# A two-block transformer kernel on one core: residual stream and output projections turned channel-major, norm factors applied after the projections

## The chip, the cores and the metric

One core of one Trainium2 chip runs the whole program. The metric is the device time of one execution in microseconds, lower is better; a kernel's time is the median of its runs.

## What is computed

256 tokens of width 1024 pass through two blocks in fp32. The first block is a token mixer (four groups of 256 channels: softmax attention with forget gates, gated delta rule, two gated linear attentions) and a convolutional gated feed-forward. The second has two layers: a short-convolution mixer or differential attention, a convolutional feed-forward, and a gated per-layer embedding. Each sub-layer has a norm before it, and those of the second block one behind it too:

```python
x = x + mixed @ w_out                                   # first block
x = x + conv_glu_ffn(rms_norm(x, norm2_g), ...)
for i in range(2):                                      # second block
    h = rms_norm(x, g_pre_mix[i])
    mix = short_conv_mixer(h, ...) if i == 0 else diff_attention(h, k, v, ...)
    x = x + rms_norm(mix, g_post_mix[i])
    ffn = conv_ffn(rms_norm(x, g_pre_ffn[i]), ...)
    x = x + rms_norm(ffn, g_post_ffn[i])
    x = x + rms_norm(sigmoid(rms_norm(x, g_pre_ple[i]) @ w_gate) * (p[i] @ w_proj), g_post_ple[i])

def rms_norm(x, g):
    return x * rsqrt(mean(x * x, axis=-1) + EPS) * g
def conv_ffn(h, w_up, w_conv, w_down):
    gate, up = split(causal_dwconv(h @ w_up, w_conv), 2)    # 3 taps along the tokens
    return (silu(gate) * up) @ w_down
```

## The kernel before, in words

**The weight stream.** All weights go through the core as 160 blocks of 128 x 2048 floats (1 MB), three slots of a ring deep. SyncE loads a block into `raw`, ScalarE copies it to `w_hi` rounded to fp32r (`split` of the scalar program, L980 to L985), VectorE makes `w_lo` = raw - w_hi (`split` of the vector program, L1459 to L1461). Every product is three fp32r matmuls: hi x hi, hi x lo, lo x hi. TensorE counts used blocks in `block_used`. Block n shares a slot with block n - 3, so ScalarE may split block n once block n - 3 is used; `ahead(n)` on both engines splits block n + 2, at a place in the program that is written out by hand. TensorE waits for both parts in `block_ready`. There is no planner: each engine's order is the order of its code.

**Two kinds of block.** A column block holds 256 columns of a weight and all 1024 of its rows; `columns` (from L400) makes 2 x 8 x 3 matmuls of 256 columns from it. A row block holds 256 rows and all 1024 columns; `row_block` (from L429) makes 2 x 2 x 3 x 2 matmuls of 512 columns, with the tokens' chunk as the weight side and the block as the moving side, so that the result lies token-major in PSUM banks 0 to 3 (`low4`), the first token tile in banks 0 and 1.

**Norms.** `x` is token-major, 2 tiles of 128 tokens by 1024. `norm` lets ScalarE square and sum tile 0 (L1011), take the factor by logarithm and exponential (L999, L1000) and scale the tile into `xn` (L1013); VectorE does tile 1 (L1472, L1475). TensorE then turns both tiles by 16 transposes (`turn`, L461), ScalarE reads them with the gain into `h_hi` (L1028) and VectorE into `h_lo` (L1489). Only then the next column block can start. Post norms (`post`) do the same with the projection in PSUM: square and sum (L1346), factor, scale with the broadcast gain (L1954), add to x (L1957), tile by tile.

**Feed-forward.** 11 pairs of a gate and an up block, each with a row block of `w_down`. The loop has three blocks per pass: gate block of pair i, up block of pair i, row block of pair i - 1. Per pair ScalarE multiplies by the last convolution tap out of PSUM (L1274), VectorE adds the two older taps out of PSUM (L1866, L1870), ScalarE applies silu (L1285), VectorE multiplies (L1893), and the product is split into high (ScalarE, L1291) and low (VectorE, L1897). Between them both engines make the splits of the coming blocks.

**Mixer.** 15 column blocks, the first of which holds only 28 columns of gates; between and in the middle of them stand hand-placed pieces of the four mixers (`before` and `middle` lists of each engine). ScalarE rounds the masks (L1047) and makes the gates beside block 1; TensorE's sums of the gates stand before block 3. Three projections get convolution taps (L1552) and are turned in the middle of block 4 (L521).

**Attention.** Blocks k (4), q (4) and v (4, row blocks), with logits, softmax and transposed weights of one head at a time in the middle of the blocks; after the last block the head products, a norm of each head (L2040) and 16 transposes before the output projection.

**GpSimd** only issues DMAs here: tables, and six broadcasts of a post gain.

## Time and profile before

| | us |
|---|---|
| Median of 3 runs | 1187.96 (1186.85 to 1188.34) |
| Time of the profiled execution, first to last instruction (span) | 1187.9 |
| TensorE matmul busy | 1088.8 |
| VectorE busy | 753.8 |
| ScalarE busy | 589.0 |
| GpSimd busy | 8.8 |
| Mean granted TensorE clock, share of full | 0.945 |

The profile is one execution taken by the hardware profiler. A busy TensorE is not one at its peak: matmuls overlap, so the distance from one start to the next says more than a duration. In the timeline a row is: start, duration, engine, line, operation, output and inputs, shapes, count, and in brackets the idle time before it with what ended it. A line may be that of a helper: L390 is every matmul but those of the row blocks, which are L445.

### The profile page before, as it was taken

The page shows a single profiled execution, that of the slowest core. Times are in us where ns is not written, and L with a number is a line of the kernel's source. Part 1 is how long each engine was busy: PE and PEld are TensorE (multiplying, and loading weights), DVE is VectorE, ACT ScalarE, POOL GpSimd, SP SyncE. Part 2 cuts the span into 40 slices and gives each one's busy share as a digit, 9 for nine tenths or more (in the row PEclk, how much of TensorE's full clock was granted, in tenths as well). Part 3 has the DMA queues.
Part 4 walks back from the last instruction along what each step waited for, and adds up shares of the span by engine and source line. Part 5 has one row for each costly group of instructions (what it writes and reads, how often), then busy time and mean ns, then how long its engine had stood idle before and what let it go on. Part 6 is the DMA issues. An engine that isn't in the chain of part 4 may idle for free.

```text
span 1187.9 us, 19600 instructions
## 1 busy us (share of the span) xinstructions
PE 1088.8 (92%) x7748; PEld 997.1 (84%) x7748; DVE 753.8 (63%) x940; ACT 589.0 (50%) x788; POOL 8.8 (1%) x20
## 2 busy tenths in 40 slices
PE   5899987889999997998999999896996899999985
PEld 5899976769999996996999999676985699999964
DVE  5765535557667666656677666746586576676673
ACT  6643242246445545444545544645564555544563
POOL 0000000000000000001000000000000000000000
PEclk9999976699999998999899999997998999999998
DMA  8333310034555553456255554442441445555530
GB/s 352 128 107 107 107 36 1 2 111 158 197 181 176 201 184 125 163 203 244 94 209 177 195 191 177 159 153 89 175 148 66 159 143 181 202 175 184 178 123 35
DMA packets 25675, 178.00 MB, mean 150 GB/s; under 512 B 2925, under 2 KB 3077, under 8 KB 5024
## 3 DMA queue, kind: packets, MB, share of 16 engines
q1 hardware_dynamic: 24208, 172.54, 40.8%
q0 software_dynamic: 1424, 4.85, 1.3%
q8 instruction: 32, 0.52, 0.2%
q14 instruction: 11, 0.09, 0.0%
HBM read 176.32 MB, written 1.06 MB: 149 GB/s over the span
## 4 chain that ended last, share of the span: by engine, by line
PE 72%; DVE 6%; ACT 3%; issue 1%; DVEq 0%
PE PS L390 43%; PE PS L445 27%; DVE h_lo L1489 1%; DVE arena L1954 1%; PE PS L461 1%; DVE x L1957 1%; DVE arena L1472 1%; PE PS L767 1%; DVE xn L1475 0%; ACT stat L999 0%; ACT arena L1346 0%; DVE w_lo L1461 0%; ACT h_hi L1028 0%; PE PS L772 0%; PE PS L830 0%
## 5 line engine op out<-in xcount | busy, mean ns | idle before, releaser
L1461 DVE TENSOR_TENSOR w_lo<-raw,w_hi 128x2048 fp32r<-128x2048 f32 x160 | 365.8, 2289 | 150.5 <-ACT w_hi L985 145.6
L390 PE MATMUL PS<-h_hi,w_hi 128*128 128x256 f32 (+1 forms) x1400 | 398.9, 285 | 5.5 <-DVE h_lo L1489 4.0
L390 PE MATMUL PS<-h_lo,w_hi 128*128 128x256 f32 (+1 forms) x1400 | 397.1, 284 | 0.0
L390 PE MATMUL PS<-h_hi,w_lo 128*128 128x256 f32 (+1 forms) x1400 | 397.1, 284 | 0.0
L985 ACT ACTIVATE w_hi<-raw 128x2048 fp32r<-128x2048 f32 x160 | 305.6, 1913 | 47.5 <-PE PS L445 43.3
L390 PEld LDWEIGHTS PS<-h_hi,w_hi 128*128 128x128 f32 (+1 forms) x1400 | 267.6, 191 | 9.1 <-issue 4.3
L390 PEld LDWEIGHTS PS<-h_lo,w_hi 128*128 128x128 f32 (+1 forms) x1400 | 267.5, 191 | 1.5
L390 PEld LDWEIGHTS PS<-h_hi,w_lo 128*128 128x128 f32 (+1 forms) x1400 | 267.3, 191 | 0.1
L1274 ACT ACTIVATE arena<-PS,channel 128x256 f32<-128x256 f32 x132 | 59.4, 501 | 168.2 <-PE PS L390 168.2
L445 PE MATMUL PS<-w_hi,act_hi 128*128 128x512 f32 x408 | 129.8, 400 | 7.3 <-DVE act_lo L1897 4.3
L445 PE MATMUL PS<-w_lo,act_hi 128*128 128x512 f32 x408 | 128.3, 396 | 0.0
L445 PE MATMUL PS<-w_hi,act_lo 128*128 128x512 f32 x408 | 128.3, 396 | 0.0
L1866 DVE SCALAR_TENSOR_TENSOR arena<-PS,channel,arena 128x255 f32<-128x255 f32 x132 | 57.6, 478 | 108.9 <-ACT arena L1274 108.7
L390 PE MATMUL PS<-arena 64*64 64x64 f32 (+7 forms) x1074 | 86.5, 290 | 13.1 <-DVE arena L1770 4.4
L445 PEld LDWEIGHTS PS<-w_hi,act_hi 128*128 128x128 f32 x408 | 74.9, 191 | 24.6 <-DVE act_lo L1897 5.6
L390 PEld LDWEIGHTS PS<-arena 64*64 64x64 f32 (+4 forms) x1074 | 72.5, 184 | 24.5 <-DVE arena L1760 5.4
L445 PEld LDWEIGHTS PS<-w_hi,act_lo 128*128 128x128 f32 x408 | 77.8, 191 | 17.3
L445 PEld LDWEIGHTS PS<-w_lo,act_hi 128*128 128x128 f32 x408 | 77.8, 191 | 17.2
L461 PE MATMUL PS<-ident,xn 128*128 128x128 f32 x160 | 29.8, 350 | 39.1 <-ACT xn L1013 18.3
L1291 ACT ACTIVATE act_hi<-arena 128x512 fp32r<-128x512 f32 x33 | 20.9, 632 | 88.1 <-PE PS L445 80.4
L1870 DVE SCALAR_TENSOR_TENSOR arena<-PS,channel,arena 128x254 f32<-128x254 f32 x132 | 57.5, 477 | 8.9 <-DVE arena L1866 0.2
L461 PEld LDWEIGHTS PS<-ident,xn 128*128 128x128 f32 x160 | 24.6, 182 | 44.6 <-ACT xn L1013 20.9
(275 smaller groups left out, 1059.8 us busy)
## 6 DMA issues: line engine op xcount, KB each, us to landing
raw<-weights SPq DMA_DIRECT2D x160, 1024.0 KB, 4.7
arena<-post_in POOLq DMA_DIRECT2D x6, 512.0 KB, 4.2
arena<-masks_in SPq DMA_DIRECT2D x1, 1856.0 KB, 15.3
x<-x_in SPq DMA_DIRECT2D x1, 1024.0 KB, 5.0
arena<-bias_by_distance POOLq DMA_DIRECT2D x1, 1024.0 KB, 9.6
result<-x SPq DMA_DIRECT2D x2, 512.0 KB, 2.7
arena<-p_in POOLq DMA_DIRECT2D x2, 256.0 KB, 8.6
row<-row_in SPq DMA_DIRECT2D x1, 390.0 KB, 11.6
```

What stands on the lines that cost most here:

```text
L390: return pe.matmul(o, lhs, rhs, start=start, stop=stop)
L445: last = pe.matmul(acc[:, t, half * 512:(half + 1) * 512], a[:, k0 + kk, tok], w[:, slot, at:at + 512], start=first and kk == 0 and j == 0 ...
L461: last = pe.transpose(PS[:, bank + j // 2, at:at + P], src[:, t, j * P:(j + 1) * P], ident[:, :])
L767: pe.matmul(o(h, t), a_la[:, la_unit(t, h), :], src(h, t), start=False, stop=False, skip_group_check=True)
L985: act.activation(w_hi[:, slot, :], raw[:, slot, :], ACT.Copy).then_inc(hi_ready, 1)
L1274: ins = act.activation(dst[:, c, :], PS[:, bank, c * TOK:(c + 1) * TOK], ACT.Identity, scale=w, bias=b)
L1291: act.activation(hid_hi, hidden, ACT.Copy).then_inc(sem("hidden_hi"), 1)
L1461: tt(w_lo[:, slot, :], raw[:, slot, :], w_hi[:, slot, :].bitcast(F), ALU.subtract).then_inc(lo_ready, 1)
L1472: dve.tensor_tensor_reduce(squares, x[:, 1, :], x[:, 1, :], 1.0, 0.0, ALU.mult, ALU.add, s) \
L1489: ins = stt(lo[:, j, :], src, gain(j), hi[:, j, :].bitcast(F), ALU.mult, ALU.subtract)
L1866: stt(y[:, c, 1:TOK], src[:, c, 0:TOK - 1], channel[:, bass.ds(col(1) + c, 1)], y[:, c, 1:TOK], ALU.mult, ALU.add).then_inc(ready[0], 1)
L1870: ins = stt(y[:, c, 2:TOK], src[:, c, 0:TOK - 2], channel[:, bass.ds(col(0) + c, 1)], y[:, c, 2:TOK], ALU.mult, ALU.add)
```

## The change

The residual `x` becomes channel-major: 8 chunks of 128 channels by 256 tokens; so do the input x, p and the result, which the host turns. All row blocks give channel-major results (`channel_rows`), with the block as the weight side and 256 token columns as the moving side. Norm factors are no longer applied before the projections. The operand is `x` times gain, split chunk by chunk (`prepare`, `chunk_lo`); the mean of squares comes from ScalarE's squares, summed by GpSimd and multiplied by a matrix of ones in full fp32, which leaves the factor of each token on every partition; VectorE multiplies each projection's output by it. The first two blocks behind a norm are taken together by chunks (`columns_by_chunk`). In the feed-forward two pairs are begun before the loop, the down block runs two pairs behind, and banks 4, 5 and 6, 7 alternate. Values of the attention become column blocks, the order of its blocks is k0 k1 q0 q1 v0 k2 q2 v1 k3 q3 v2 v3, heads are multiplied out in pairs, their norm uses a matmul of ones, and GpSimd scales the first softmax map. In the mixer, the small block (now 114 KB) and block 1 are computed together, the gates' TensorE sums move from before block 3 to its middle, and ScalarE's and VectorE's part of the gates from block 1 to block 2. TensorE:

```diff
+            def columns_by_chunk(p, n0, banks, operand):
+                a_hi, a_lo = operand
+                for k in range(KC):
+                    for lo in range(2):
+                        pe.wait_ge(lo_chunk if lo else hi_chunk, chunk_at(p, k))
+                        for j, bank in enumerate(banks):
+                            slot = (n0 + j) % RING
+                            if k == 0 and lo == 0:
+                                block_ready(n0 + j)
+                            for f in range(2):
...
+            def channel_rows(n0, slot, operand, k0, first, final, bank_of=lambda c: c // 2, signal=True, at_chunk=None):
+                block_ready(n0)
+                a_hi, a_lo = operand
+                for c in range(KC):
...
+                    for kk in range(2):
+                        at = kk * D + c * P
+                        ws_hi, ws_lo = w_hi[:, slot, at:at + P], w_lo[:, slot, at:at + P]
+                        add(o, ws_hi, a_hi[:, k0 + kk, :], first and kk == 0 and c % 2 == 0)
+                        add(o, ws_hi, a_lo[:, k0 + kk, :])
+                        last = add(o, ws_lo, a_hi[:, k0 + kk, :], False, final and kk == 1)
+                    if final and signal and c in (1, 3, 5):
+                        last.then_inc(bank_summed, 1)
+                last.then_inc(block_used, 1)
+            def mean_of_x(p, bank, total, by_token=False):
+                pe.wait_ge(sem("x_sum"), p + 1)
+                for half in range(2):
+                    last = add(PS[:, bank, 0:TOK], ones[:, :], total[:, half * TOK:(half + 1) * TOK], half == 0, half == 1)
...
-            turn("norm2", xn, tile_ready=2)
-            ffn(0, "norm2")
+                columns_by_chunk(p, n0, (4, 5), (h_hi, h_lo))
+                mean_of_x(p, 0, sum_x)
+                columns(n0 + 2, slot(2), 6, (h_hi, h_lo))
+                columns(n0 + 3, slot(3), 7, (h_hi, h_lo))
+                def triple(n, at, pairs_done, odd, first=False):
+                    bank = 6 if odd else 4
+                    pe.wait_ge(sem("gate_read"), pairs_done)
+                    columns(n, slot(at), bank, (h_hi, h_lo))
+                    pe.wait_ge(sem("up_read"), pairs_done)
+                    columns(n + 1, slot(at + 1), bank + 1, (h_hi, h_lo))
+                    pe.wait_ge(sem("hidden_split"), pairs_done)
+                    channel_rows(n + 2, slot(at + 2), hid[odd], 0, first, False)
+                triple(n0 + 4, 4, PAIRS * f + 1, 0, True)
+                with pe.Fori(1, 5) as i:
...
```

ScalarE and VectorE at the head of the feed-forward (the vector side has the same order, with `read` the scaling read of a bank into `z_gate` or `z_up`):

```diff
+                ahead(n0)
+                ahead(n0 + 1)
+                rstd_x(p, 0, r_x[:, 0:TOK])
+                gate(0)
+                ahead(n0 + 2)
+                up(0)
+                hid_part(0, 0)
+                ahead(n0 + 3)
+                gate(1)
+                up(1)
+                hid_part(1, 1)
+                if f:
+                    act.activation(p_hi, p_tok, ACT.Copy).then_inc(sem("p_hi"), 1)
+                triple(2, n0 + 4, 0, 0, 0)
...
+                ahead(n0)
+                ahead(n0 + 1)
+                dve.wait_ge(sem("x_rstd"), p + 1)
+                read(z_gate, 4, sem("gate_read"), 0, n0 + 1)
+                gate(0)
+                read(z_up, 5, sem("up_read"), 0, n0 + 2)
+                ahead(n0 + 2)
+                up(0)
+                hid_part(0, 0)
+                ahead(n0 + 3)
+                read(z_gate, 6, sem("gate_read"), 1, n0 + 3)
+                gate(1)
+                read(z_up, 7, sem("up_read"), 1, n0 + 4)
+                up(1)
+                hid_part(1, 1)
...
+                def triple(q, n_base, step, i, odd):
+                    split_of(n_base + 2, step, i)
+                    read(z_gate, bank, sem("gate_read"), q, n_base + 1 + step * i)
+                    gate(q)
+                    split_of(n_base + 3, step, i)
+                    read(z_up, bank + 1, sem("up_read"), q, n_base + 2 + step * i)
+                    up(q)
+                    split_of(n_base + 4, step, i)
+                    hid_part(q, odd)
```

The adds of the residual, and the start and the gates of the mixer:

```diff
+                update(0)
+                update(1)
+                chunk_lo(u + 1, 0)
+                update(2)
+                update(3)
+                chunk_lo(u + 1, 1)
+                ahead(n_used - 1)
+                chunk_lo(u + 1, 2)
...
+            first_columns()
+            mean_of_x(0, 6, sum_1, True)
...
-            before = {3: [gates], 6: [gdn_channels], 7: [gdn_turn_decay], 14: [gdn_solve]}
-            middle = {1: [turn_small], 3: [gk_product], 4: [gdn_tokens], 6: [gdn_grams], 7: [gdn_turn_m], 8: [la_turn_keys], 14: [fox_turn]}
+            before = {6: [gdn_channels], 7: [gdn_turn_decay], 14: [gdn_solve]}
+            middle = {2: [turn_small], 3: [gates, gk_product], 4: [gdn_tokens], 6: [gdn_grams], 7: [gdn_turn_m], 8: [la_turn_keys], 14: [fox_turn]}
...
+                tt(pair(4 + n % 2), pair(4 + n % 2), units(r_1, 2), ALU.mult).then_inc(sem("gdn_scaled"), 1)
```

In the embedding stage ScalarE makes all chunks of the operand, then a copy of bank 7, then `ahead(n - 1)`, the split of the second gate block. In the attention it runs, beside the last value block, `values(2)`, `soften(7)`, `copy_weights(5)`, while TensorE's middle of that block is `logits(7)`, `turn_weights(5)`, `heads_out(2)`, the last of which waits for that copy.

## Rows read from the trace of the kernel before

**Rows 1.** The page's first part: busy us (share of the span), instructions.

```profile
PE 1088.8 (92%) x7748; PEld 997.1 (84%) x7748; DVE 753.8 (63%) x940; ACT 589.0 (50%) x788; POOL 8.8 (1%) x20
```

**Rows 2.** Windows by stage: length, busy us (instructions) of engines, clock, DMA share, GB/s.

```profile
0.00:263.30 263.30, 228.35 (x2006) 207.78 (x2006) 144.99 (x224) 112.08 (x161) 2.63 (x10) 0.87 0.29 107
263.30:458.80 195.50, 190.86 (x1341) 178.50 (x1340) 135.72 (x156) 104.74 (x117) 0.00 (x0) 1.00 0.50 177
458.80:560.30 101.50, 96.55 (x691) 90.85 (x690) 61.04 (x58) 44.66 (x50) 2.71 (x4) 0.97 0.52 184
560.30:760.80 200.50, 193.46 (x1346) 181.37 (x1346) 139.03 (x161) 104.48 (x126) 0.56 (x1) 0.98 0.51 177
760.80:796.80 36.00, 31.73 (x137) 25.54 (x135) 18.53 (x19) 19.28 (x26) 0.54 (x1) 0.91 0.43 154
796.80:939.70 142.90, 122.87 (x752) 106.22 (x752) 91.85 (x141) 78.13 (x151) 1.24 (x2) 0.92 0.35 124
939.70:1140.00 200.30, 193.71 (x1346) 181.64 (x1346) 139.04 (x161) 104.47 (x126) 0.56 (x1) 0.98 0.51 177
1140.00:1175.50 35.50, 31.26 (x137) 25.17 (x135) 17.42 (x19) 15.71 (x24) 0.53 (x1) 0.95 0.09 37
1175.50:1187.90 12.40, 0.00 (x0) 0.00 (x0) 6.15 (x5) 5.49 (x10) 0.00 (x0) 0.68 0.21 85
```

**Rows 3.** TensorE's waits from 263 us on: us in total, times, longest.

```profile
PE PS L461 <- ACT xn L1013: 18.3, 5, 6.2
PE PS L445 <- DVE h_lo L1489: 7.1, 2, 3.5
PE PS L461 <- DVE xn L1475: 5.9, 7, 1.3
```

**Rows 4.** TensorE's timeline over one pass of a feed-forward loop.

```profile
298.35 0.28 PE L390 MATMUL PS<-h_hi,w_hi 128*128 128x256 f32 x1
...
309.87 0.63 PE L445 MATMUL PS<-w_hi,act_hi 128*128 128x512 f32 x2
...
315.38 0.28 PE L390 MATMUL PS<-h_hi,w_hi 128*128 128x256 f32 x1
```

**Rows 5.** The chain that ended last, at the last embedding norm's low parts.

```profile
1148.53 3.24 DVE h_lo L1489 x8
```

**Rows 6.** The timeline's full-fp32 matmuls of 512 columns; four, recorded as eight.

```profile
797.91 3.70 PE L390 MATMUL PS<-arena 128*128 128x512 f32 x8 [1.11 <-ACT arena L1365]
```

**Rows 7.** Timeline of ScalarE and VectorE over a feed-forward's first pair.

```profile
577.46 0.84 ACT L1274 ACTIVATE arena<-PS,channel 128x256 f32<-128x256 f32 x2 [4.50 <-PE PS L390]
...
578.34 0.87 DVE L1866 SCALAR_TENSOR_TENSOR arena<-PS,channel,arena 128x255 f32<-128x255 f32 x2 [3.05 <-ACT arena L1274]
...
580.21 2.29 DVE L1461 TENSOR_TENSOR w_lo<-raw,w_hi 128x2048 fp32r<-128x2048 f32 x1
...
585.91 0.69 DVE L1893 TENSOR_TENSOR arena<-arena 128x512 f32<-128x512 f32 x1
586.63 0.63 ACT L1291 ACTIVATE act_hi<-arena 128x512 fp32r<-128x512 f32 x1 [2.57 <-DVE arena L1893]
...
587.29 0.69 DVE L1897 TENSOR_TENSOR act_lo<-arena,act_hi 128x512 fp32r<-128x512 f32 x1 [0.70 <-ACT act_hi L1291]
```

**Rows 8.** Timeline: the logits of one attention head on TensorE.

```profile
862.50 0.93 PE L390 MATMUL PS<-arena 64*128 64x256 f32 x8
```

**Rows 9.** Timeline of the start: x, first matmul, masks, gates, third projection's transposes.

```profile
5.74 1.06 ACT L1011 ACTIVATE arena<-x 128x1024 f32<-128x1024 f32 x1 [3.71 <-DMA x<-x_in]
...
9.19 0.47 PE L461 MATMUL PS<-ident,xn 128*128 128x128 f32 x1 [9.19 <-DMA channel<-channel_in]
...
24.47 1.80 ACT L1047 ACTIVATE level_masks<-arena 128x1920 fp32r<-128x1920 f32 x1
...
30.94 0.28 PE L390 MATMUL PS<-arena,level_masks 128*128 128x4 f32 x2
...
47.36 1.12 PE L521 MATMUL PS<-ident,arena 128*128 128x128 f32 x4 [1.26 <-ACT arena L1077]
```

1512 lines of the change are left out of this document (887 added, 625 removed).

## The prediction, made before the changed kernel was run

> **What bounds the kernel now.** I read the busy shares first: TensorE is busy for 92% of the span, VectorE 63%, ScalarE 50% [rows 1]. Then the busy time by stage, cut where the last matmul of each projection ends [rows 2]; the nine stretches add up to the span. The three feed-forward stages (second, fourth and seventh row) have TensorE busy for all but 5 to 7 us of about 200, at full clock. The others lose more: 20 us in the 142.9 of embedding gate plus attention, 35 in the mixer (its clock is 0.87), all of the 12.4 us tail. The waits of TensorE [rows 3] say what a transition between stages costs: it waits for ScalarE to scale the first token tile, then for VectorE's second tile or for the low parts of the operand. So TensorE is the bound inside the stages, and the chain square, factor, scale, transpose, split is the bound between them. The profiled execution's span is 1187.9 us; its own time and the median of the three runs (1187.96) are the same to 0.1 us, so sums against 1187.9 hold for the median.
>
> **Part 1, row blocks turned channel-major.** One pass of the feed-forward loop has 96 matmuls of 256 columns from 298.35 to 309.87, 0.120 us each, and 24 of 512 columns up to 315.38, 0.230 us each [rows 4]. A column block is 48 x 0.120 = 5.76 us, a row block 24 x 0.230 = 5.51 us. The change makes all 59 row blocks (16 in three output projections and the value projection, 33 down, 2 + 8 in the embedding stages) into 48 matmuls of 256 columns: +0.25 us x 59 = **+15 us**, all on the path, spread over the stages below. The Trainium skill, "TensorE: Matmul & The Clock Gate", section "Back-to-back issue gap", gives columns / 2.4 GHz plus 2.5 ns per matmul; by that a block would grow by only 0.06 us and the 59 by 3.5 us. The rows decide, since a pass measures both widths in this kernel.
>
> **Part 2, transitions after a residual alone (before the first feed-forward stage and the short convolution).** The transposes, the factor and the scaling leave the path. The bank of the last projection is summed two chunks at a time, VectorE adds 256 columns in 0.41 us (as the splits do, 3.24 us for 8 [rows 5]), ScalarE makes the high part meanwhile, and TensorE starts two blocks at once, chunk by chunk. Only the split of the second block (2.29 us of VectorE, put in the middle of the adds) holds it, about 0.5 us. The two blocks take 11.5, the mean of squares by a matmul of ones in full fp32 0.93 (four 512-column ones take 3.70 [rows 6], here two of 256). The short-convolution stage is then 0.5 + 11.5 + 0.9 + 14 x 5.76 + 0.7 (the table product, as before) = 94.3 for 101.5: **-7.2**. VectorE's work per three blocks there is about 14.4 us under 17.3, so nothing else waits.
>
> **Part 3, the feed-forward ramp.** This is the term that decides. After the mean matmul TensorE runs on into blocks 3 to 6 of the stage, 4 x 5.76 = 23.0 us, and then needs block 7. The split of block 7 stands on both ScalarE and VectorE behind the whole handling of pairs 0 and 1. Counting from the end of the mean matmul: factor 1.5, split of block 4 until 2.95; then for pair 0 read and scale 0.65, last tap 0.84 and hand-over 0.1, four taps 1.9, second read 0.65, a split 2.25 (the second last tap lies beside it), taps 1.9, product 0.7, high part 0.75, low part 0.7 = 10.4; split of block 6, whose high part (1.91) starts only after the pair's high part, 3.4; pair 1 without a split inside 9.1; split of block 7 3.4. Sum 29.3, against 23.0: TensorE waits 6.3 us, and 0.8 more in the next two blocks until the steady order is reached. The durations are those of one pair and its splits in the kernel before, 577.46 to 587.98 [rows 7]; what is new there is two reads of the 512-column kind. In the stages with the per-layer input its own split (0.63 and 0.69) adds 0.7. After the ramp VectorE needs 15.5 us per triple under TensorE's 17.3, so the loop stays TensorE's. The wait also costs clock: a stage that begins with a wait of TensorE has a mean granted clock of 0.98 and one without 1.00 [rows 2]; 0.02 of 200 us, had every such stretch run at 1.2 instead of 2.4 GHz with work to do, is 4 us. I take 1.2, between 0 and 4. First stage: 0.5 + 11.5 + 0.9 + 31 x 5.76 + 7.1 + 1.2 = 199.8 for 195.5, **+4.3**.
>
> **Part 4, transitions with a post norm.** TensorE sums the squares (four fp32 matmuls of 256, done 1.9 after the projection), factor 1.1, then VectorE scales, adds and splits eight chunks in 9.4 us; lo parts come every 0.8 to 1.5 us while TensorE wants one per 1.44. Two blocks are done 16.5 after the projection, mean 17.4, ramp 7.8, clock 1.2, 31 blocks 178.6: 205.0 for 200.5 and 200.3, **+4.6 each**. Embedding stages: TensorE runs the projection beside the post norm, but the second gate block's split waits behind ScalarE's eight chunks and a bank copy, 3.8 us; 36.5 for 36.0 and 35.5, **+1.5** together. Tail: five sigmoids and products by banks, table back (1.28), squares, eight ones-matmuls of 0.46 until 7.1, factor 1.0, 13 VectorE steps 6.0, last quarter stored 2.6: about 17 for 12.4, **+4.5**. Before, five steps of 1.2 us on VectorE did it for both token tiles, and half the result was on its way while the second tile was added.
>
> **Part 5, embedding gate to attention output.** The same chain, but the bias flip (3.7 [rows 6]) fills TensorE: the two key blocks are done at 22 after the gate's last matmul, and the query block, whose split waits behind sixteen high parts and the bias copy on ScalarE, starts at 24.5. Ten blocks 57.6; eight logits of about 0.9 [rows 8], transposes, head products and three new fp32 means 17; the output projection with its last head pair 26. The copy of head 5's weights stands behind the exponentials of head 7, while TensorE waits for it in the middle of the last value block: 6. With 1.5 for clock that is 132.6, for 142.9: **-10**. The saving is the square, factor, scale and transpose chain before and after the heads, where TensorE is busy for only 122.9 of 142.9 us now [rows 2].
>
> **Part 6, the start.** All of x (1 MB) is there at 5.74 [rows 9]; the second block's weights come after half of x and the small block, 1.7 MB in all, so near 7.4. High and low part take 1.9 + 2.3, so TensorE, which wants both blocks' weights at the first chunk, starts at 11.7 instead of 9.2 [rows 9], runs both blocks in 10.3 (partly at half clock) and the mean in 1.4: 23.4. But the gates and their mask copy (1.80 [rows 9]) now stand behind that factor, two splits and the scaled taps: ready near 38, while TensorE asks in the middle of the fourth block, at 32, and everything behind that wait in its queue stands too. Before it ran them at 30.94 with no wait [rows 9]. The third convolution's taps follow the same chain and its transposes come at 54.8 instead of 47.36 [rows 9]: +7.4. From there TensorE is full until 155, so nothing is won back; +1 for extra scaling on VectorE, +1 for the four row blocks: **+9.4**.
>
> Costed at nothing: GpSimd's sums of squares, wanted 5 us or more after their inputs in each stage; if they took longer than that they would move the factor. No row has such an instruction; the nearest, VectorE's 0.69 for 512 columns [rows 7], bounds three from below at 2.1. The Trainium skill, "GPSIMD Engine Reference", section "Performance versus the Vector engine", has 4.5 us for 2048 columns with two inputs, an estimate of 3.4 for three. No run here shows it yet. The broadcasts of the post gains leave GpSimd's queue and the DMA engines, which are busy for half of a feed-forward stage [rows 2] and hold nobody up there.
>
> **Sum.** 9.4 + 4.3 - 7.2 + 4.6 + 4.6 + 1.5 - 10 + 4.5 = +11.7: **1199.6 us**. Bounds of the unknowns: start 0 to +11, each ramp 3 to 10 with clock, attention -16 to -4, tail +2 to +6: 1182 to 1214.
>
> **Rivals.** (A) *The ramp is covered, and the kernel is faster.* If the chain of Part 3 takes 23 us or less between mean and split of block 7 (if ScalarE's taps from SBUF are quicker, or splits slip ahead), all three ramps vanish with their clock cost: 3 x 8.8 = -26, 1173. It decides where 29.3 falls under 23.0. For it: VectorE is only 63% busy [rows 1]. Against: the chain is made of hand-overs in a fixed order, which a low busy share does not shorten. If the start is covered too, 1165. (B) *Gains and costs cancel*, the start and half of each ramp hidden: about 1188. (C) *DVE falls behind in the loop too*: if a triple took 18.3 instead of 15.5, each of the 27 triples behind the ramps would give 1 us: 1227. Against: steps counted above. (D) *The row blocks cost only 3.5 us*, the wider cadence of rows 4 being due to what stands between blocks: 1199.6 - 11.5 = 1188.
>
> **How the numbers follow.** About 0.2% (2.4 us) is what a measurement of this kernel can tell from no change. Forecast 0.56, A 0.28, B with D 0.10, C 0.06. The forecast's own range is 1190 to 1212; with A the range is 1166 to 1212, leaving out C and the far end of A. Faster 0.32 (A and part of B), same 0.08, slower 0.60.
>
> **What would show it.** The changed kernel's timeline must show 5.76 us for each block of a projection; in each feed-forward stage a wait of TensorE of 5 to 8 us for VectorE's w_lo, before the first down block; under 1 us between the mixer's projection and the next stage; a wait for the gates near 32; a 5 us wait in the last value block; and the tail 17 us long. If the w_lo waits are missing, Part 3 is wrong and A holds. If stages two, four and seven are under 192 us, the sum's sign is wrong.

## The result, and the profile after

The changed kernel takes 1220.8 us (median of 4 runs, 1220.4 to 1221.6), the kernel before 1188.2 (1186.9 to 1189.6): 1.0275 times as long, 95% interval 1.026 to 1.029. The forecast was 1199.6, range 1166 to 1212: the sign was right, the size was not, and the time lies outside the range. The profiled execution's span is 1219.0 us, so 19.4 us are to be found.

The page's first part of the changed kernel; it answers to [rows 1]. TensorE is busy for 25 us more, VectorE for 59 us more, GpSimd now computes:

```profile
PE 1113.7 (91%) x9104; PEld 1081.4 (89%) x9104; DVE 813.1 (67%) x1099; ACT 598.8 (49%) x781; POOL 63.1 (5%) x55
```

The windows by stage of the changed kernel, cut at the same places of the work as [rows 2]: the stretch and its length, then busy us (instructions) of PE, PEld, DVE, ACT, POOL, the granted clock, the DMA share, GB/s:

```profile
0.00:274.10 274.10, 233.58 (x2099) 217.75 (x2100) 150.10 (x230) 112.93 (x166) 8.84 (x16) 0.86 0.28 101
274.10:474.90 200.80, 193.84 (x1591) 193.30 (x1590) 149.71 (x182) 106.62 (x115) 5.26 (x4) 0.97 0.50 173
474.90:569.20 94.30, 94.12 (x775) 92.88 (x773) 62.99 (x65) 41.84 (x41) 5.82 (x5) 1.00 0.51 180
569.20:775.70 206.50, 197.18 (x1597) 195.63 (x1596) 153.88 (x191) 107.22 (x123) 4.59 (x4) 0.98 0.51 174
775.70:815.20 39.50, 34.44 (x253) 33.72 (x252) 26.66 (x33) 20.91 (x28) 4.32 (x3) 0.91 0.37 134
815.20:956.80 141.60, 125.31 (x932) 116.90 (x932) 83.29 (x170) 79.53 (x150) 25.89 (x19) 0.94 0.35 120
956.80:1161.80 205.00, 195.67 (x1597) 194.06 (x1596) 153.78 (x191) 106.97 (x123) 4.04 (x3) 0.98 0.49 169
1161.80:1201.10 39.30, 34.28 (x252) 33.59 (x252) 24.37 (x31) 17.53 (x27) 4.32 (x3) 0.91 0.08 28
1201.10:1219.00 17.90, 5.29 (x16) 3.61 (x16) 8.27 (x18) 5.20 (x10) 0.00 (x0) 0.74 0.16 59
```

Stage by stage against the forecast (lengths in us; the forecast is before plus its term):

| stage | before | forecast | after | after - forecast |
|---|---|---|---|---|
| mixer | 263.3 | 272.7 | 274.1 | +1.4 |
| feed-forward 0 | 195.5 | 199.8 | 200.8 | +1.0 |
| short convolution | 101.5 | 94.3 | 94.3 | 0.0 |
| feed-forward 1 | 200.5 | 205.1 | 206.5 | +1.4 |
| both embedding stages | 71.5 | 73.0 | 78.8 | +5.8 |
| gate to attention output | 142.9 | 132.9 | 141.6 | +8.7 |
| feed-forward 2 | 200.3 | 204.9 | 205.0 | +0.1 |
| tail | 12.4 | 16.9 | 17.9 | +1.0 |

Six of the eight rows are within 1.4 us. Two are not: the attention, which was to win 10 us and won 1.3, and the embedding stages, which were to lose 1.5 and lost 7.3. They are 14.5 of the 19.4 us.

TensorE's waits from 258 us on in the changed kernel (us in total, times, longest), which answer to [rows 3]:

```profile
PE PS L473 <- DVE w_lo L1663: 29.3, 7, 6.8
PE PS L473 <- ACT arena L1551: 9.4, 2, 8.7
PE PS L473 <- ACT xn L1528: 5.5, 4, 2.1
PE PS L473 <- ACT h_hi L1136: 5.1, 2, 2.5
PE PS L438 <- DVE w_lo L1663: 4.6, 2, 3.4
```

The waits for a scaled token tile are gone. In their place TensorE waits 33.9 us for splits of weight blocks (L1663) and 8.7 us at one place in the attention for a copy (L1551). Here are the first of the ramps, the second gate block of an embedding stage and that place in the attention, in TensorE's timeline of the changed kernel (start, us, instruction; in brackets the idle time before it and what ended it):

```profile
316.87 0.55 PE L473 MATMUL PS<-act_hi,w_hi 128*128 128x256 f32 x1 [6.78 <-DVE w_lo L1663]
...
794.24 0.55 PE L473 MATMUL PS<-h_hi,w_hi 128*128 128x256 f32 x1 [4.97 <-DVE w_lo L1663]
...
923.11 1.19 PE L473 MATMUL PS<-arena 128*128 128x256 f32 x2 [8.72 <-ACT arena L1551]
```

A wait costs more than its length. Windows of the changed kernel around the wait at 794 show the granted clock at its lower level (0.51 is 1.2 GHz of 2.4) for 6.9 us, most of it after the wait, while TensorE had work; the same stands around 317, where 10.2 us are at 0.50:

```profile
786.00:793.20 7.20, 3.27 (x28) 3.07 (x26) 6.68 (x8) 6.17 (x8) 3.42 (x3) 1.00 0.00 0
793.20:800.10 6.90, 5.86 (x27) 5.89 (x28) 5.30 (x3) 2.17 (x2) 0.00 (x0) 0.51 0.71 258
800.10:808.00 7.90, 7.90 (x65) 7.79 (x64) 1.56 (x1) 2.69 (x3) 0.00 (x0) 1.00 0.46 175
...
312.00:322.20 10.20, 5.33 (x25) 5.37 (x26) 7.20 (x8) 5.92 (x6) 0.00 (x0) 0.50 0.30 103
```

TensorE was busy for 5.3 and 5.9 us of these stretches, with 25 and 27 matmuls. At the 0.120 us from one start to the next of a full clock [rows 4] these take 3.0 and 3.2 us, so about 2.3 and 2.6 us went on top of waits of 6.8 and 5.0.

### The profile page after: what moved, and what is told of

Read it like the earlier page. It is cut to its first block, busy times and chain, and to the rows that moved or that the text cites. A ratio compares the mean times of both kernels' runs of the same rounds, so it can differ in the third digit from the quotient of the medians.

```text
span 1219.0 us, 22148 instructions
## 1 busy us (share of the span) xinstructions
PE 1113.7 (91%) x9104; PEld 1081.4 (89%) x9104; DVE 813.1 (67%) x1099; ACT 598.8 (49%) x781; POOL 63.1 (5%) x55
## 4 chain that ended last, share of the span: by engine, by line
PE 59%; DVE 12%; ACT 7%; issue 2%; POOL 1%; DVEq 0%; ACTq 0%
PE PS L438 29%; PE PS L473 28%; DVE w_lo L1663 3%; ACT w_hi L1119 3%; DVE x L2103 2%; POOL arena L428 1%; DVE h_lo L1676 1%; DVE arena L2152 1%; DVE arena L2097 1%; DVE arena L2156 1%; ACT arena L1541 1%; ACT arena L1420 1%; PE PS L869 1%; ACT arena L1542 0%; DVE arena L2170 0%
## 5 line engine op out<-in xcount | busy, mean ns | idle before, releaser
L1663 DVE TENSOR_TENSOR w_lo<-raw,w_hi 128x2048 fp32r<-128x2048 f32 x159 | 363.2, 2287 | 111.9 <-ACT w_hi L1119 110.4
L438 PE MATMUL PS<-h_hi,w_hi 128*128 128x256 f32 x1248 | 357.5, 286 | 8.0 <-DVE w_lo L1663 4.6
L438 PE MATMUL PS<-h_lo,w_hi 128*128 128x256 f32 x1248 | 355.6, 285 | 0.0
L438 PE MATMUL PS<-h_hi,w_lo 128*128 128x256 f32 x1248 | 355.4, 285 | 0.0
L438 PEld LDWEIGHTS PS<-h_hi,w_hi 128*128 128x128 f32 x1248 | 242.1, 194 | 9.4 <-issue 3.9
L438 PEld LDWEIGHTS PS<-h_lo,w_hi 128*128 128x128 f32 x1248 | 242.1, 194 | 0.1
L438 PEld LDWEIGHTS PS<-h_hi,w_lo 128*128 128x128 f32 x1248 | 242.0, 194 | 0.0
L473 PE MATMUL PS<-act_hi,w_hi 128*128 128x256 f32 x720 | 206.3, 288 | 21.1 <-DVE w_lo L1663 19.0
L473 PE MATMUL PS<-h_hi,w_hi 128*128 128x256 f32 (+1 forms) x344 | 99.1, 301 | 28.2 <-DVE w_lo L1663 16.5
L473 PE MATMUL PS<-h_hi,w_lo 128*128 128x256 f32 (+1 forms) x344 | 96.9, 294 | 0.0
L473 PE MATMUL PS<-h_lo,w_hi 128*128 128x256 f32 (+1 forms) x344 | 82.9, 295 | 0.1
## 6 DMA issues: line engine op xcount, KB each, us to landing
arena<-masks_in SPq DMA_DIRECT2D x1, 1856.0 KB, 12.4
```

The costliest lines, as they stand in the source:

```text
L438: return pe.matmul(o, lhs, rhs, start=start, stop=stop)
L473: return pe.matmul(o, lhs, rhs, start=start, stop=stop, skip_group_check=True)
L1663: tt(w_lo[:, slot, :], raw[:, slot, :], w_hi[:, slot, :].bitcast(F), ALU.subtract).then_inc(lo_ready, 1)
```

## The experiments

All are edits of the changed kernel, and none leaves work out. In the diffs of e1, e2, e9 and e13 statements that stand on lines of their own are put on one line, and only a part of each edit is shown. Medians, with the ratio to the kernel before (run on the same chip, 1187.7 to 1189.3) and its 95% interval:

| | us | ratio to before |
|---|---|---|
| changed kernel | 1220.8 | 1.0275 (1.026 to 1.029) |
| e1 splits first | 1213.4 | 1.020 (1.017 to 1.022) |
| e2 copy 5 first | 1215.9 | 1.023 (1.020 to 1.025) |
| e3 scaling on VectorE | 1220.5 | 1.026 (1.024 to 1.029) |
| e4 sums on VectorE | 1220.5 | 1.026 (1.024 to 1.029) |
| e5 reads first | 1196.6 | 1.007 (1.005 to 1.009) |
| e6 one gate split | 1215.3 | 1.024 (1.022 to 1.025) |
| e7 e2 + e3 | 1217.1 | 1.025 (1.023 to 1.026) |
| e8 taps first | 1218.3 | 1.026 (1.024 to 1.028) |
| e9 attention order | 1218.4 | 1.026 (1.023 to 1.028) |
| e10 gate order | 1209.2 | 1.018 (1.016 to 1.020) |
| e11 e5, e8, e9, e10 | 1179.8 | 0.993 (0.991 to 0.995) |
| e12 e11 + e3 + e4 | 1173.4 | 0.988 (0.985 to 0.991) |
| e13 attention, all orders | 1214.1 | 1.022 (1.020 to 1.024) |
| e14 gate, all orders | 1208.0 | 1.017 (1.015 to 1.018) |
| e15 e11 + e3 | 1179.5 | 0.992 (0.991 to 0.994) |
| e16 all | 1165.4 | 0.980 (0.979 to 0.982) |
| e17 e16, sums on GpSimd | 1167.2 | 0.983 (0.981 to 0.985) |
| e18 e16, scaling on GpSimd | 1165.9 | 0.982 (0.979 to 0.984) |

The mixer's length alone, which most of these edits do not touch, differs by up to 3 us between profiled executions, so the stage lengths of the profiles say more than differences of 2 us between medians. The changed kernel was timed once, before all of these; the kernel before was timed again with each group and stayed within 0.2%.

**e1 and e5: the ramp is a debt of order.** e1 makes four splits earlier and lets the pair work run one pair later:

```diff
-                up(0); hid_part(0, 0); ahead(n0 + 3)
-                gate(1); up(1); hid_part(1, 1)
+                up(0); ahead(n0 + 3); hid_part(0, 0); ahead(n0 + 4)
+                gate(1); ahead(n0 + 5); up(1); ahead(n0 + 6); hid_part(1, 1)
```

> The three feed-forward ramps: the splits of blocks 5, 6, 7 and 8 of a stage are made ahead of the pair work they stood behind, on ScalarE and VectorE; the pair work runs one pair later until pairs 9 and 10. Theory R (the ramp is a debt of one pair of work, which the loop pays back at 17.3 - 15.5 = 1.8 us per triple, and the wait also costs clock): the waits of 6.78, 6.75 and 5.44 us before the first down block go, and with them the half-clock stretch behind each (about 2.7 us each): -25 us, 1196. Rival M (the wait is only moved: another w_lo is as late one or two blocks on, since the same work stands ahead of it): waits of 3 to 6 us before block 7 or 8 of each stage, 1210 to 1221.

Measured: 1213.4, which lies in M's range. The waits before the first down block are gone, as R had it, but in each stage one came before the last down block (M had looked for it before block 7 or 8). TensorE's timeline of e1:

```profile
465.23 0.58 PE L473 MATMUL PS<-act_hi,w_hi 128*128 128x256 f32 x1 [4.54 <-DVE act_lo L2202]
```

The lag of a pair was still there at the end. As I read it (argued, not tried by itself), the loop's spare 1.8 us per triple went into waits for a free slot of the ring, behind which the pair work stood. e5 adds two things: the read of a bank ahead of a split, on VectorE alone, and on both engines a lag that shrinks by one split a pair from pair 7 on. The first:

```diff
+                    read(z_gate, bank, sem("gate_read"), q, n_base + 1 + step * i)
                     split_of(n_base + 5, step, i)
-                    read(z_gate, bank, sem("gate_read"), q, n_base + 1 + step * i)
                     gate(q)
```

> As the first experiment, and VectorE reads a bank (0.68 us) ahead of a split instead of behind it, so that ScalarE's last tap runs beside the split and VectorE no longer idles 1.2 us for it twice a pair; the lag of a pair is worked off from pair 7 on, one split a pair. Theory R (what a feed-forward stage loses is the ramp's debt: the first experiment had no wait at the ramp and one of 4.54, 3.67 and 3.30 us before the last down block instead, its end): no wait over 0.5 us in any of the three stages, their granted clock at full, each stage 191 to 193 us for 200.8, 206.5 and 205.0 less 9: in all -25 to -29 us against the changed kernel's 1220.8, so 1192 to 1196. Rival M (VectorE's work per triple really exceeds what the loop pays back, so that a wait shows in another place): 1203 to 1213.

Measured: 1196.6, 24.2 under the changed kernel. Windows of e5 over the three feed-forward stages:

```profile
275.30:466.60 191.30, 191.12 (x1591) 190.84 (x1590) 148.94 (x182) 106.35 (x115) 5.25 (x4) 1.00 0.53 182
...
560.90:758.40 197.50, 194.83 (x1597) 193.64 (x1596) 153.03 (x191) 106.51 (x123) 4.59 (x4) 0.99 0.53 182
...
940.60:1138.10 197.50, 194.85 (x1596) 193.67 (x1596) 153.03 (x190) 106.37 (x123) 4.02 (x3) 0.99 0.51 176
```

200.8, 206.5 and 205.0 became 191.3, 197.5 and 197.5: TensorE idles 0.2 us of the first. Theory R holds; a ramp cost 9.5, 9.0 and 7.5 us, of which 6.8 (5.4 in the last) are the wait. Which of e5's two additions took away e1's new wait is not told apart.

**e2, e7, e9, e13: the attention's waits move from place to place.** e2 swaps two lines of ScalarE:

```diff
-            soften(7); copy_weights(5)
+            copy_weights(5); soften(7)
```

> On ScalarE the copy of head 5's turned weights stands ahead of head 7's exponentials instead of behind them. Theory O (TensorE's wait of 8.72 us in the last value block is this order: the copy waits for the exponentials of head 7, which wait for head 7's logits to be read at 920.6): the copy is made near 917.3, the head product starts 5.4 us earlier, and 1.4 us of clock come back: -5 to -7 us, 1214 to 1216. Rival H (head 7's own chain decides when the second output block can go on): the gain is given back before the output projection's second block, under 2 us, 1219 to 1221.

Measured: 1215.9; the stage from the gate to the attention output took 136.3 us for 141.6. Theory O, at its lower end: a wait of 2.88 us stayed, for the same copy, now behind a split.

> The second experiment (1215.9) and the third together: the copy of head 5's weights ahead of head 7's exponentials, and the scaling of the first softmax map on VectorE. Theory G (GpSimd's 2.90 us beside a split lies in the chain of every head; alone the third experiment could not show it, since TensorE waited 8.7 us for something else): the remaining wait of 2.88 us before the head product goes: -2 to -4 us against 1215.9, so 1212 to 1214. Rival N (the chain of a head has slack of more than 3 us wherever TensorE waits): 1215 to 1216.5.

Measured: 1217.1, no better than e2, and the wait was 3.43. G was wrong here, and N, the nearer one, still a little too low.

e9 moves copy and values ahead of the split too, and at the start splits the query block before the eight query chunks:

```diff
-            ahead(a0 + 11); values(2); soften(7); copy_weights(5)
+            values(2); copy_weights(5); ahead(a0 + 11); soften(7)
```

> Attention alone: on ScalarE values 2 and the copy of head 5's weights stand ahead of the split of the block after next (in the second experiment they stood behind it, and TensorE still waited 2.88 us); at the start the query block is split ahead of the eight query chunks. Theory O (what is missing from the forecast's -10 us here is order): the wait in the last value block falls from 8.72 to about 1 us with its half-clock stretch, the wait at the query block from 3.36 to about 2: stages six and seven together 133 to 135 us for 141.6, so 1212 to 1214. Rival W (the work itself is what the forecast had too low): 136 or more, 1216 or more.

Measured: 1218.4, worse than e2, with the stage at 139.3 us: by its numbers this is W. But the wait for the copy fell to 1.08 us as expected, and a new one stood behind it. TensorE's waits of e9 from the gate to the attention output:

```profile
PE PS L438 <- ACT xn L1564: 3.8, 1, 3.8
PE PS L438 <- DVE h_lo L2309: 3.0, 1, 3.0
```

L1564 is the square of the third head pair, which stood behind head 7's exponentials as well. So e9 alone does not tell O from W. e13 moves that square too, lets the query block wait for its low parts chunk by chunk, and has e3 in it:

```diff
-            soften(7); head_squares(2)
+            head_squares(2); soften(7)
```

> Attention alone, all its orders: as the ninth, with the squares of the third head pair ahead of head 7's exponentials, the query block waiting chunk by chunk, and the scaling on VectorE. Theory O (the attention's missing 9 us are waits that ScalarE's order makes): no wait over 1.7 us from the query block to the attention output, the two stages 131 to 134 us for 141.6, so 1210 to 1213. Rival W (the work was estimated too low, the waits only move): 137 or more, 1216 or more.

Measured: 1214.1, a little above the expected 1210 to 1213, but the stage took 132.8 us. Its window over the whole stage, and behind it the changed kernel and e13 from the query block's start on:

```profile
815.20:948.00 132.80, 125.09 (x932) 115.61 (x932) 86.25 (x186) 79.07 (x150) 4.02 (x3) 0.97 0.37 128
...
841.80:956.80 115.00, 104.76 (x800) 99.16 (x800) 61.26 (x133) 60.58 (x117) 21.86 (x16) 0.93 0.40 138
...
840.40:948.00 107.60, 102.84 (x800) 96.79 (x800) 67.88 (x156) 62.91 (x119) 0.00 (x0) 0.98 0.43 147
```

TensorE is busy for 125.1 us, as in the changed kernel (125.3), and idle for 7.7 instead of 16.3. W is wrong: what was missing was the order, of ScalarE above all. That 132.8 meets the forecast's 132.9 is partly luck, since the forecast had 7.5 us of wait and clock in it. Without these it had 125.1 us; e13 still idles 4.8 us behind the query block's start and loses about 1.6 to the clock (3.4 us of work at its lower level), which leaves about 126.4. So the work was forecast about 1 us too low, no more. e13 joins four edits. The place of the scaling is not the one that matters: e18 below has it on GpSimd, and the stage takes 130.8 us.

**e6, e10, e14: the embedding stages.** e6 makes the split of the second gate block behind four chunks of the pre norm, on both engines:

```diff
+                    if p in (4, 7) and b == 1:
+                        ahead(STEP["ple_gate0" if p == 4 else "ple_gate1"] - 1)
```

> In both embedding stages the split of the second gate block is made behind chunks 0 to 3 of the pre norm, instead of behind all eight chunks and the copy of a projection bank. Theory O (TensorE's waits of 4.97 and 4.95 us there are this order, and each costs 3.4 us more since the granted clock is at half for the 6.9 us from 793.2 to 800.1 and from 1179.0 to 1185.8): the waits go, the stages take 31 to 33 us for 39.5 and 39.3: -13 to -17 us, 1204 to 1208. Rival C (the chunks 4 to 7 come 2.3 us later by the split put ahead of them, and the third gate block waits instead): stages of 36 to 38, -3 to -6 us, 1215 to 1218.

Measured: 1215.3, in C's range, with stages of 34.7 and 36.2 us, between the two. TensorE now waited 2.07 us for the third gate block's split, behind the bank copy. e10 moves that one too, and squares the products of banks 1 and 2 ahead of ScalarE's table reload instead of behind it:

```diff
-                    if p in (4, 7) and b == 1:
+                    if p in (4, 7) and b in (1, 2):
...
+                        if b == 3:
+                            product_squares(layer, q + 1, half + 1)
...
                         act.preload_act_table_set(TABLES)
-                        for part in range(1, 5):
+                        for part in range(3, 5):
```

> Embedding stages and tail alone: the splits of the second and the third gate block are made behind chunks 3 and 5 of the pre norm (the sixth experiment moved only one and left a wait of 2.07 us for the other); the squares of products 2 to 6 are made ahead of the reload of ScalarE's table instead of behind it. Theory O: no wait over 1 us in the gate blocks, stages of 32 to 34 us for 39.5 and 39.3; the attention's start and the tail 2 to 3 us earlier as TensorE's fp32 sums start earlier: -14 to -18 us, 1203 to 1207. Rival C (the chunks come later by the splits, TensorE waits for these): 1211 to 1215.

Measured: 1209.2, between the two ranges; stages of 35.0, tail 15.2 for 17.9. The splits no longer hold TensorE; its wait was 2.9 us for GpSimd's last addition (releaser POOL arena L398), since the mean of squares stood behind the second gate block. e14 puts it behind the third (`if j == 2` for `if j == 1`).

> Embedding stages alone: as the tenth, with TensorE's mean of squares behind the third gate block instead of the second. Theory O: the wait of 2.89 us for GpSimd's last addition goes in both, stages of 32 us for 35.0: -5.5 us against 1209.2, 1203 to 1205. Rival F (the factor then comes too late for the reads of the gate banks and the tail grows by as much): 1208 to 1210.

Measured: 1208.0 (1205.7 to 1208.7). Windows of e14: both embedding stages and, between them, the attention, which this edit leaves alone:

```profile
774.40:806.60 32.20, 32.09 (x253) 31.21 (x252) 21.41 (x28) 18.99 (x25) 4.01 (x3) 1.00 0.37 131
806.60:950.60 144.00, 127.05 (x932) 118.21 (x932) 85.58 (x173) 81.13 (x153) 25.89 (x19) 0.93 0.36 125
1156.60:1188.70 32.10, 32.07 (x252) 31.22 (x252) 21.64 (x30) 17.38 (x27) 4.00 (x3) 1.00 0.10 34
```

The stages are down from 39.5 and 39.3 to 32.2 and 32.1, TensorE full at 1.00. But the attention behind the first took 144.0, for 141.2 in e10: all that the first stage gained against e10 is lost again, since TensorE waits 3.41 us for the products' squares there (1.88 in the changed kernel). Behind the second stage the tail stayed at 15.2, so that gain was kept. The time of 1208.0 is F's; O holds in the lengths of the stages and in the second one's gain.

**e3, e4, e12, e15, e17, e18: GpSimd and VectorE exclude each other, and in most orders it costs little.** The timeline of VectorE and, in the second pair of rows, of GpSimd in the changed kernel, at the attention's start and beside a split of head 0:

```profile
827.75 0.47 DVE L2103 SCALAR_TENSOR_TENSOR x<-arena,channel,x 128x256 f32<-128x256 f32 x1
828.14 1.51 DVE L1676 SCALAR_TENSOR_TENSOR act_lo<-x,channel,act_hi 128x256 fp32r<-128x256 f32 x1
...
827.98 1.40 POOL L394 TENSOR_TENSOR arena<-xn 128x512 f32<-128x512 f32 x1 [36.98 <-ACT xn L1137]
...
861.52 2.90 POOL L428 TENSOR_SCALAR arena<-arena 128x256 f32<-128x256 f32 x1 [25.74 <-DVE arena L2355]
864.41 0.59 POOL L429 TENSOR_SCALAR arena<-arena 128x128 f32<-128x128 f32 x1
```

VectorE's operation (L1676) takes 1.51 us where the same took 0.47 elsewhere in the norm, and GpSimd's scaling, 0.92 us in the later heads, takes 2.90 beside VectorE's split (2.29, unchanged). 21 of VectorE's operations are stretched so, by 21.4 us in all (not 26 and 26.6, as the expectation of e4 has it). The Trainium skill, "SBUF — State Buffer", section "Who interferes with whom", says that a VectorE instruction with two SBUF inputs and a GpSimd instruction that reads SBUF exclude each other, the second waiting for the whole of the first. These rows agree: the split began at 861.33 and ended at 863.62, and 0.92 us more make 864.54, where the scaling ended at 864.42. e3 takes the scaling to VectorE, e4 the additions:

```diff
-                dve.wait_ge(sem("att_scaled"), h + 1)
+                mark(ts(l1[:, 0, :], l1[:, 0, :], a[:, 8:9], None, ALU.mult))
+                mark(ts(l0[:, 0, :], l0[:, 0, :], a[:, 10:11], None, ALU.mult))
...
+                if c in (5, 6, 7):
+                    add_squares(p, c - 4)
```

> VectorE scales the first softmax map of each head itself, just ahead of combining the two maps; GpSimd does nothing in the attention. Theory G (GpSimd and VectorE exclude each other: GpSimd's scaling takes 2.90 us beside VectorE's split and 0.92 alone, and both wait for the result): per head 3.5 us (heads 0 to 3 and 6) or 1.5 us (the others) of hand-over become 0.5 to 0.6 us; what of it lies on the path is head 6, ahead of head 7's logits being read: -2 to -4 us, 1217 to 1219. Rival N (the scaling is covered by other work and its time on VectorE is added): 1220 to 1223.

> VectorE adds the squares of each norm (three additions of 512 columns, 2.1 us a norm) behind its low parts of chunks 5, 6 and 7; GpSimd adds nothing. Theory G (whenever GpSimd adds, VectorE's operation of 0.47 us beside it takes 1.50: 26 times 1.03 us = 26.6 us in all, three or four times in each norm): VectorE's chain in a norm gets shorter by about 3.1 - 2.1 = 1 us; on the path in the two embedding stages, the attention's start and the mixer's start: -3 to -6 us, 1215 to 1218. Rival N (the stretched operations lie beside work of TensorE, and the 2.1 us come on top of the chain): 1221 to 1226.

Measured: 1220.5 and 1220.5, e3 within N and e4 just under it. The stretched operations lie where TensorE has work or waits longer for something else. Whether they would cost when the other waits are gone was asked four times.

> All orders together: fifth, eighth, ninth and tenth experiment. If the waits are separate, the sum -24 - 2.5 - 7 - 15 = -48.5: 1172, and 1170 to 1176, ahead of the kernel before (1188) by 1.0 to 1.5%. If they overlap or new waits come, 1176 to 1184.

> The eleventh with GpSimd's additions and scalings on VectorE, as in the third and fourth experiment. Theory G in its last form (VectorE's operations of 0.47 us take 1.50 beside GpSimd's additions; the third, fourth and seventh experiment gained nothing since other waits lay in the same places; with those gone it shows): 2 to 6 us under the eleventh. Rival N (2.1 us more of VectorE's own work per norm cost as much as they save): within 1.5 us of the eleventh, either way.

> The eleventh (1179.8) with the attention's scaling on VectorE and the sums of squares still on GpSimd. The twelfth, with both on VectorE, took 1173.4. If the scaling in the chain of a head is what GpSimd costs: 1174 to 1175.5. If it is the sums, which stretch VectorE's operations to 1.5 us in each norm: 1178 to 1179.5.

Measured: e11 1179.8, e12 1173.4, e15 1179.5. e11 is faster than before by 0.7%, but gained 41.0 us, not 48.5: the attention took 137.9 us, where the sum needed 134.6 (its new wait of 3.8 us was in it), and each embedding stage 36.5 for e10's 35.0. The medians of e12 and e15, read by the expectations, say that the sums cost and the scaling does not. The stages say more. The attention (gate to output) took 137.9 us in e11, 135.3 in e15 and 132.7 in e12: each part of GpSimd's work that left gave about 2.6 us there. e15's median hides it, since its mixer was 2.3 us longer than e11's. Windows of e11 and e15 over the part of the attention behind the query block's start, where e15's gain lies:

```profile
815.90:863.50 47.60, 46.67 (x363) 45.27 (x364) 29.17 (x67) 25.86 (x51) 13.94 (x8) 0.94 0.44 149
...
818.20:863.40 45.20, 45.13 (x363) 43.76 (x363) 31.66 (x75) 25.96 (x51) 0.00 (x0) 0.97 0.49 168
```

0.9 us of it are idle time, TensorE's waits for the combined maps of a head, and 1.5 are busy time at a lower clock. What the sums gave lies in the wait for VectorE's low parts at the query block (3.25 us in e15, 1.91 in e12) and in that for the third head pair's squares (4.40 and 2.75). So G holds for the attention in e11's order, by one profiled execution each. With these waits gone too:

> The sixteenth (1165.4) with the sums of squares back on GpSimd. Theory G (each addition on GpSimd stretches VectorE's operation beside it from 0.47 to 1.5 us): where TensorE follows VectorE's chunks closely, at the attention's start and in the embedding stages, 1 to 3 us each, in the feed-forward and short-convolution transitions nothing: 1168 to 1171. Rival N: 1165 to 1166.5.

> The sixteenth (1165.4) with the scaling of the first softmax map back on GpSimd, where it takes 3.5 us beside a split and 1.5 us alone, for 0.6 on VectorE. Theory G: head 6's and 7's hand-overs lie ahead of TensorE's second and third output block: 1167 to 1170. Rival N (every head has that slack): 1165 to 1166.5.

Measured: 1167.2 (1165.8 to 1168.4) and 1165.9 (1164.8 to 1166.3), against e16's 1165.4 (1164.5 to 1166.3): e17 between its two ranges, e18 in N's. The sums may cost 1.8 us, at the edge of what these runs can tell; the scaling costs nothing that they can. In e18's profile the attention is even 1.5 us shorter than in e16's (130.8 for 132.3), with TensorE's clock full in all of it. In the profile of e17 every stage from feed-forward 0 on is as long as in e16 within 0.4 us. The exclusion has a price only where TensorE waits for VectorE's chain.

**e8: the mixer's start.** In the changed kernel TensorE waits at 35.52:

```profile
35.52 0.58 PE L438 MATMUL PS<-h_hi,w_hi 128*128 128x256 f32 x1 [3.47 <-DVEq L1657]
```

L1657 is VectorE's signal that block 1's bank is read by the convolution taps. e8 does those taps ahead of the split of block 3, on both engines:

```diff
-                ahead(n)
+                if n > 1:
+                    ahead(n)
...
                 if 1 <= n <= 3:
                     gdn_taps(n - 1, n)
+                if n == 1:
+                    ahead(n)
```

> In the mixer, behind the first factor, ScalarE and VectorE do the convolution taps of block 1 ahead of the split of block 3. Theory S (TensorE's wait of 3.47 us ahead of block 3 at 35.5 is for the bank that the taps read until 35.4, behind a split of 2.3 us that waits 1.8 us for its high part; everything behind it moves along): block 3 starts 1.8 us earlier, the gates and the third taps 1 to 2 us earlier, half-clock time shorter: -1.5 to -3 us, 1218 to 1219. Rival D (block 3's own split then comes as late): 1220 to 1221.

Measured: 1218.3, within S, but its interval overlaps the changed kernel's; block 3 now waits 2.36 us, for its own split, instead of 3.47 for the bank. The profiles of all kernels say more than these medians. The next stage starts at 272.8 to 275.8 us (mean 274.5) in the twelve without this edit and at 270.3 to 273.3 (mean 271.5) in the seven that have it. The gain at the start is about 3 us, rather at S's upper end.

**e16: everything together**, e12 with e13's and e14's edits.

> The twelfth (1173.4) with the edits of the thirteenth and fourteenth. Sum of the waits that go: 2.75 and 1.9 in the attention, 2.6 twice in the embedding stages, 3 of half clock: 1161 to 1165. If they move: 1168 to 1173.

Measured: 1165.4 us, just above the first range, 0.9805 of before (0.979 to 0.982) and 55 us under the changed kernel. Windows of e16 from feed-forward 0 to the tail:

```profile
271.50:462.80 191.30, 191.12 (x1590) 190.84 (x1590) 147.82 (x185) 106.35 (x115) 0.00 (x0) 1.00 0.54 182
462.80:557.10 94.30, 94.12 (x774) 92.86 (x773) 61.85 (x68) 41.83 (x41) 1.44 (x2) 1.00 0.53 180
557.10:754.60 197.50, 194.82 (x1597) 193.74 (x1596) 152.97 (x194) 106.51 (x123) 0.56 (x1) 0.99 0.54 182
754.60:786.80 32.20, 32.05 (x253) 31.21 (x252) 23.15 (x32) 18.90 (x25) 0.00 (x0) 1.00 0.39 132
786.80:919.10 132.30, 124.52 (x933) 115.48 (x932) 88.50 (x192) 80.92 (x153) 0.00 (x0) 0.97 0.40 136
919.10:1116.50 197.40, 194.80 (x1597) 193.68 (x1596) 152.86 (x193) 106.50 (x123) 0.00 (x0) 0.99 0.51 176
1116.50:1148.80 32.30, 32.12 (x253) 31.22 (x252) 23.51 (x35) 17.44 (x27) 0.00 (x0) 1.00 0.10 33
```

Against [rows 2] every one of these stages is shorter than before, by 34.9 us together. The mixer (271.5 for 263.3) and the tail (15.1 for 12.4) stay longer, by 10.9. With the orders of e16 the change gains about 2%; with the orders it came with it loses 2.75%. How much the kernel before would gain if its own orders were written again was not tried, so the 2% are not shown to be the structure's alone.

## Why the prediction was right or wrong

**Part 1, the row blocks: right.** The loop pass of the changed kernel, in TensorE's timeline:

```profile
325.04 0.28 PE L438 MATMUL PS<-h_hi,w_hi 128*128 128x256 f32 x1
...
336.55 0.28 PE L473 MATMUL PS<-act_hi,w_hi 128*128 128x256 f32 x1
...
342.31 0.28 PE L438 MATMUL PS<-h_hi,w_hi 128*128 128x256 f32 x1
```

17.27 us for 17.03 in [rows 4], and the down block 342.31 - 336.55 = 5.76 as forecast. Rival D would have had it at 5.57; these rows refuse it. Its 3.5 us came from the formula of the Trainium skill, "TensorE: Matmul & The Clock Gate", section "Back-to-back issue gap". That section of the Trainium skill gives the formula as the gap of a matmul by itself, and says that in a stream of weight loads and matmuls the spacing is another. For the stream here the formula does not hold: the trace shows 0.120 us for 256 columns, where it gives 0.109.

**Part 2, the transition after a residual: right to 0.1 us.** The short-convolution stage took 94.3 us for 94.3.

**Part 3, the ramp: right in mechanism and place, low in its clock term.** The wait was to be 6.3 and 0.8 us and is 6.78; before the first down block, for w_lo, as the text asked. "I take 1.2, between 0 and 4" for the clock is where it was low: 2.3 at the first, by its matmuls. The rows that it was read from did not compare a wait with none: before, the stages at 0.98 begin with a wait of 4.6 us, the one at 1.00 with two of 1.5 and 1.4. A ramp cost 9.5, not 8.3. Rival A had priced the disappearance of all three at 26 us; e5, which makes them disappear, gained 24.2. Rival C is refused by the pass of 17.27.

**Part 4, post norms: feed-forwards right, embedding stages wrong.** The wait in the gate blocks was named with its cause and put at 3.8 us; it was 4.97, and it was given no clock at all, though 2.6 us were lost to it. "+1.5 together" was +7.3. The term that was mis-sized is the wait: 1.2 of it and about 2.5 of clock, twice, is 7.4, more than the 5.8 missing. The rest of a stage was put too high: 32.7 us without the wait, where e14 shows 32.2 and 32.1. Tail: 17.9 for 17.

**Part 5, the attention: the step that failed.** "-10" was -1.3. The work was right within about 1 us (e13). The wait at head 5's copy was foreseen, with its cause, at 6 us, and 1.5 for clock. It was 8.72 us. The chain at that place, in the timelines of GpSimd, VectorE and ScalarE:

```profile
916.27 2.53 POOL L429 TENSOR_SCALAR arena<-arena 128x128 f32<-128x128 f32 x1
...
918.84 0.48 DVE L2364 SCALAR_TENSOR_TENSOR arena<-arena 128x256 f32<-128x256 f32 x1 [0.50 <-POOL arena L429]
...
920.73 0.51 ACT L1541 ACTIVATE arena<-arena 128x256 f32<-128x256 f32 x1 [3.99 <-DVE arena L2346]
...
922.50 0.47 ACT L1551 ACTIVATE arena<-PS 128x384 f32<-128x384 f32 x1
```

The chain that was not followed to its end: the copy (L1551) stands behind head 7's exponentials (L1541), these wait for head 7's logits to be read, the reads stand on VectorE behind the combination of head 6's maps (L2364), and that waits for GpSimd's scaling (L429) beside a split. The logits were read at 920.6, where TensorE asked for the copy at 914.4. The query block started 26.6 us after the gate, not 24.5. Its wait of 3.36 us and that of 8.72 were each followed by TensorE's work at half clock, 6.1 and 3.3 us of it, which cost about 4.3 us for the 1.5 forecast. Against the 132.6 that Part 5 adds up to, that is 2.1 us at the query block's start, 4.2 of idle time behind it (10.2 for 6) and 2.8 of clock, which covers the 9.0 missing. And it was taken as one wait to be counted, where e9 shows that behind it stood the next.

**Part 6, the start: size nearly right, mechanism partly not.** +10.8 for +9.4. First full matmul at 13.41 (forecast 11.7), since the second block's weights were there at 9.03, not at 7.4; third transposes at 56.69 (54.8). No wait for the gates at 32: TensorE had waited 3.47 us for block 1's bank before, so that the gates, ready at 39.7, were there when it came to them at 39.97. A bank that a slow reader holds was not in the forecast.

**GpSimd "costed at nothing": right for the changed kernel (e3 and e4 moved it by 0.4 us), and for a reason not given.** Most additions take 1.3 to 1.5 us, not the 0.7 of the lower bound. That GpSimd's work would stretch VectorE's was not seen; only the spare time around it made the zero right. In e11's order the same work cost 6.4 us by the medians, 5.2 of it in the attention (e12), in e16's at most about 2 (e17, e18).

**The range.** It ended at 1212, where the upper bounds of the terms add up to 1212 to 1214; the lower bounds add up to about 1165, not to the 1182 of the text. Start, ramps and tail stayed inside their bounds. The attention's bound ended at -4, and it gained 1.3; the embedding stages had no bound at all, and lost 7.3. Seven waits outside the mixer (three ramps, two gate blocks, the query block, the head product) were followed by work at half clock. Counted as above, by the matmuls that ran in it, this cost about 15.5 us, where the forecast had 5.1 (three times 1.2, and 1.5). With the difference, an estimate, it would have stood near 1210, still inside the range, and with what the waits themselves fell short (6.3 in the attention, 1.2 twice in the embedding stages) near 1219.

## What to carry to other kernels

When a change moves work off the bound engine's path, the order of the engines that feed it must be written for the new path before the change is judged: here the same mathematics is 2.75% slower with one and 2% faster with the other. In a forecast, give each long wait of TensorE a second price for the clock behind it, read from windows around a wait of the same kernel. When a wait is removed, look for what stood behind it in the same queue before counting the gain, and put the reads of PSUM ahead of the long operations, so that another engine's part of the chain runs beside them (e5, though not tried by itself).

## What was not expected of the hardware

- VectorE with two inputs from SBUF and GpSimd take turns: 0.47 us becomes 1.51 beside GpSimd's addition (1.3 to 1.4), GpSimd's 0.92 becomes 2.90 beside VectorE's split (2.29). e4, which takes the 21.4 us of stretching away and puts 16.4 us of VectorE's own additions in its place, moved the time by nothing that it could show.
- A wait of TensorE of 5.0 us was followed by a granted clock of 0.51 until 800.1, with 5.9 us of work in that stretch; a wait of 6.8 us by one of 0.50 until 322.2. Without such waits the first feed-forward stage (e5) and the embedding stages (e14) stand at 1.00.
